# A kernel of two transformer blocks: the first modulation summed on TensorE by quarters of the channels

## Chip, cores and metric

One core of one Trainium2 chip. The metric is the device time of one execution in microseconds.

## What is computed

The input x (256 tokens by 1024 channels, float32) goes through two blocks: the first has a mixer of three branches (windowed attention, a gated recurrence, block attention) and a gated feed-forward layer, the second has differential attention, a Fourier mix, a dense feed-forward layer and eight experts. What the change touches is the very beginning:

```python
mod = silu(c) @ w_mod + b_mod          # c: 1024 numbers, w_mod: 1024 x 6144
shift_m, scale_m, ... = split(mod, 6)  # 1024 numbers each
h = rms_norm(x, norm_mix) * (1.0 + scale_m) + shift_m
z = h @ w_in                           # w_in: 1024 x 7424
```

So nothing of `z` can be finished before the first 2048 columns of `w_mod` (8 MB) have been read and multiplied by silu(c), while a partial sum of `z` over some input channels needs the scale and shift of these channels alone.

## The kernel before

There are 8 blocks of 128 channels, c = 0 to 7, and x lies transposed in `X`. Every weight matrix passes once through the chip, in slabs of 1 MB. SyncE issues all slab loads in one order (`st_order`, L535) into `raw` buffers. A load waits until its buffer's last slab is used. For a slab of a product (kind G, 1024 rows by 256 columns), ScalarE makes a rounded copy `whi` (`act_hi`, L1351), VectorE the rest `wlo = raw - whi` (`dve_lo`, L1969), and TensorE multiplies in three products (L663 to L665): 48 instructions for each slab of `w_in`. Three buffers of `whi` and `wlo` (NP = 3) let ScalarE and VectorE run up to three slabs ahead.

The modulation comes in slabs of kind M (512 rows by 512 columns, two to a group g of 512 outputs). `dve_mslabs` (L1991, L1994) multiplies the rows by silu(c) into an accumulator `macc`, and `pe_mods` (L741) sums that over the partitions into a column of the bank. `dve_mods` (L2012) adds the bias and puts it into `modT`. Groups 2 and 3 are the scale, groups 0 and 1 the shift. Only group 0 is summed by TensorE straight from the raw slab (`pe_mod_direct`, L755, with the 128x128 weights as the stationary operand and one column of silu(c) as the moving one).

The order of loads is: two slabs of group 2, x, two of group 3, two of group 0, two of group 1, then slabs 0, 1, 2 of `w_in`, then a slab of `w_in` and one of the next modulation in turn. On TensorE: transposes of x (L799), sums of squares for the norm (L768, L771), group 3 (L741), group 0 (L755), group 1, 14 multiplications that only keep the array busy (`spare`, L699), then `pe_mixer`: jobs 0 and 1 of `z` ("qa"), `pe_z_side(1)` (transposes L853, L859, the norm of job 0, L865), and from job 2 on one job, its side work and `pe_mods` in turn. Job 2 is "kv" (keys and values, 72 instructions), job 3 "qc" (48).

VectorE scales X (`scaled`, L2033), ScalarE adds the shift and rounds to `HH` (L1393), VectorE makes the rest `HL` (`low`, L2040). TensorE waits for `HL` of each block of channels (`xlo_done`). The loop of `dve_mixer` then makes `wlo` of slab t + 3, normalizes job t - 1 (L2245) and calls `dve_mslabs`.

## Time and profile before

| what | value |
|---|---|
| median of 3 runs | 2033.34 us (2030.17 to 2034.3) |
| the profiled execution | 2030.57 us, its span 2028.5 us |
| TensorE busy | 1980.4 us, 98% of the span |
| VectorE, ScalarE busy | 1702.0 us, 1257.4 us |
| read from memory | 585.89 MB, 289 GB/s over the span |

The span goes from the first to the last instruction. The profiled execution has its own time, 2.1 us over its span. Slabs count as 1 MB = 1.0486 million bytes here.

### The profile page before, as it was taken

The page shows a single profiled execution, that of the slowest core. Times are in us where ns is not written, and L with a number is a line of the kernel's source. Part 1 is how long each engine was busy: PE and PEld are TensorE (multiplying, and loading weights), DVE is VectorE, ACT ScalarE, POOL GpSimd, SP SyncE. Part 2 cuts the span into 40 slices and gives each one's busy share as a digit, 9 for nine tenths or more (in the row PEclk, how much of TensorE's full clock was granted, in tenths as well). Part 3 has the DMA queues.
Part 4 walks back from the last instruction along what each step waited for, and adds up shares of the span by engine and source line. Part 5 has one row for each costly group of instructions (what it writes and reads, how often), then busy time and mean ns, then how long its engine had stood idle before and what let it go on. Part 6 is the DMA issues. An engine that isn't in the chain of part 4 may idle for free.

```text
span 2028.5 us, 32745 instructions
## 1 busy us (share of the span) xinstructions
PE 1980.4 (98%) x13665; PEld 1771.3 (87%) x13665; DVE 1702.0 (84%) x1874; ACT 1257.4 (62%) x1269; POOL 39.5 (2%) x77
## 2 busy tenths in 40 slices
PE   7999999999999999999999999999999999999997
PEld 6889999999879899999878888888888888888886
DVE  6797888998786778887479898898988989898997
ACT  3469735654344554343367777777777777777775
POOL 3010000000000000000000000000000000000000
PEclk8999999999999999999999999999999999999999
DMA  9974876878643459999259999999999999999994
GB/s 310 302 248 138 264 235 224 263 235 277 219 165 105 146 194 332 320 322 324 84 208 368 368 354 371 350 374 361 362 361 355 369 352 370 367 354 369 368 372 158
DMA packets 337577, 589.16 MB, mean 290 GB/s; under 512 B 10518, under 2 KB 150316, under 8 KB 337425
## 3 DMA queue, kind: packets, MB, share of 16 engines
q1 hardware_dynamic: 333776, 580.70, 81.6%
q0 software_dynamic: 3008, 5.78, 1.0%
q8 instruction: 111, 1.82, 0.4%
q10 hardware_dynamic: 640, 0.52, 0.1%
q14 instruction: 42, 0.34, 0.1%
HBM read 585.89 MB, written 1.07 MB: 289 GB/s over the span
## 4 chain that ended last, share of the span: by engine, by line
PE 86%; DVE 8%; issue 3%; ACT 2%; DMA 1%; SPq 0%; DVEq 0%; ACTq 0%
PE bk L669 15%; PE bk L671 15%; PE bk L670 15%; PE bk L663 10%; PE bk L664 10%; PE bk L665 10%; DVE wlo L1969 2%; DVE macc L1994 2%; PE bk L1214 1%; ACT whi L1351 1%; DMA raw<-in_w_mod 1%; DVE uc L2349 1%; PE bk L1263 1%; PE bk L1126 1%; PE bk L725 1%
## 5 line engine op out<-in xcount | busy, mean ns | idle before, releaser
L1969 DVE TENSOR_TENSOR wlo<-raw,whi 128x2048 fp32r<-128x2048 f32 x477 | 1080.3, 2267 | 204.5 <-ACT whi L1351 203.2
L1351 ACT CAST whi<-raw 128x2048 fp32r<-128x2048 f32 x477 | 903.7, 1895 | 376.6 <-PE bk L671 249.0
L663 PE MATMUL bk<-HH,whi 128*128 128x256 f32 x1480 | 420.6, 284 | 0.9 <-DVE KC L2245 0.4
L664 PE MATMUL bk<-HL,whi 128*128 128x256 f32 x1480 | 410.4, 277 | 0.0
L665 PE MATMUL bk<-HH,wlo 128*128 128x256 f32 x1480 | 409.0, 276 | 0.0
L669 PE MATMUL bk<-whi,xh 128*128 128x512 f32 x896 | 354.4, 396 | 0.0
L671 PE MATMUL bk<-wlo,xh 128*128 128x512 f32 x896 | 349.3, 390 | 0.0
L670 PE MATMUL bk<-whi,xl 128*128 128x512 f32 x896 | 349.0, 390 | 0.0
L663 PEld LDWEIGHTS bk<-HH,whi 128*128 128x128 f32 x1480 | 276.9, 187 | 6.6 <-issue 3.8
L664 PEld LDWEIGHTS bk<-HL,whi 128*128 128x128 f32 x1480 | 279.6, 189 | 1.1 <-issue 0.7
L665 PEld LDWEIGHTS bk<-HH,wlo 128*128 128x128 f32 x1480 | 276.9, 187 | 0.0
L1994 DVE SCALAR_TENSOR_TENSOR macc<-raw,csil,macc 128x512 f32<-128x512 f32 x273 | 205.0, 751 | 10.2 <-DMA raw<-in_w_mod 1.8
L671 PEld LDWEIGHTS bk<-wlo,xh 128*128 128x128 f32 x896 | 168.2, 188 | 35.8
L669 PEld LDWEIGHTS bk<-whi,xh 128*128 128x128 f32 x896 | 168.3, 188 | 34.2 <-DVE wlo L1969 1.3
L670 PEld LDWEIGHTS bk<-whi,xl 128*128 128x128 f32 x896 | 168.4, 188 | 33.4
L669 PE MATMUL bk<-whi,tth 128*128 128x512 f32 x448 | 174.5, 390 | 0.7 <-DVE wlo L1969 0.7
L671 PE MATMUL bk<-wlo,tth 128*128 128x512 f32 x448 | 174.4, 389 | 0.0
L670 PE MATMUL bk<-whi,ttl 128*128 128x512 f32 x448 | 174.3, 389 | 0.0
L663 PE MATMUL bk<-FH,whi 128*128 128x256 f32 x400 | 113.2, 283 | 2.1 <-DVE wlo L1969 2.1
L664 PE MATMUL bk<-FL,whi 128*128 128x256 f32 x400 | 111.6, 279 | 0.0
L665 PE MATMUL bk<-FH,wlo 128*128 128x256 f32 x400 | 111.1, 278 | 0.0
L669 PEld LDWEIGHTS bk<-whi,tth 128*128 128x128 f32 x448 | 84.1, 188 | 18.5 <-DVE wlo L1969 1.1
(378 smaller groups left out, 2465.2 us busy)
## 6 DMA issues: line engine op xcount, KB each, us to landing
raw<-in_moe_w SPq DMA_DIRECT2D x334, 1024.0 KB, 6.5
raw<-in_ada_w SPq DMA_DIRECT2D x56, 1024.0 KB, 5.6
raw<-in_ff_w SPq DMA_DIRECT2D x40, 1024.0 KB, 5.9
raw<-in_w_in SPq DMA_DIRECT2D x29, 1024.0 KB, 5.5
raw<-in_w_mod SPq DMA_DIRECT2D x24, 1024.0 KB, 5.7
raw<-in_w_up SPq DMA_DIRECT2D x22, 1024.0 KB, 5.1
raw<-in_attn_w_qkv SPq DMA_DIRECT2D x12, 1024.0 KB, 5.6
raw<-in_w_branch SPq DMA_DIRECT2D x8, 1024.0 KB, 5.2
```

Of the source, the lines that this page charges most:

```text
L663: pe.matmul(o, sh, mh, start=start, stop=False, skip_group_check=True)
L664: pe.matmul(o, sh, ml, start=False, stop=False, skip_group_check=True)
L665: return pe.matmul(o, sl, mh, start=False, stop=stop, skip_group_check=True)
L669: pe.matmul(o, sh, mh, start=start, stop=False, skip_group_check=True)
L670: pe.matmul(o, sl, mh, start=False, stop=False, skip_group_check=True)
L671: return pe.matmul(o, sh, ml, start=False, stop=stop, skip_group_check=True)
L725: pe.matmul(o, xh[:, k, c], h[:, k, :], start=(k == 0), stop=False)
L1126: t = pe.matmul(u.t[:, m * S:(m + 1) * S], FN[:, tb, g + m, part * 128:part * 128 + 128], fcs[:, 256 + tb * 512 + part * 256:512 + tb * 51 ...
L1214: t = pe.transpose(u.t[:, j * 128:(j + 1) * 128], HB[s_ % 2][:, j * 128:(j + 1) * 128], ident)
L1351: act.copy(halves_at(q, g)[0], raw[q.slot[i]][:, :n]).then_inc(q.hi_done.mark(g), 1)
L1969: dve.tensor_tensor(low, raw[q.slot[i]][:, :n], high.bitcast(F), ALU.subtract).then_inc(q.taken.mark(i), 1)
L1994: t = dve.scalar_tensor_tensor(out=acc[:, :], in0=v[:, j, :], scalar=sc, in1=acc[:, :], op0=ALU.mult, op1=ALU.add)
```

## The change

`w_mod`'s first 2048 columns are now read in eight slabs of 1024 rows by 256 columns (kind D), as `w_in` is: quarter q holds the scale (w = 0) and the shift (w = 1) of channel blocks 2q and 2q + 1. x is loaded ahead of all slabs, and slab q of `w_in` between quarters q and q + 1, for q = 0, 1, 2. TensorE sums each slab (`pe_rows`): eight multiplications with silu(c), repeated over 32 columns (`c32`), as the stationary operand and 256 columns of the slab as the moving one; they write to four groups of 32 partitions in turn. ScalarE copies the bank (128x512) to `rowsum`, TensorE turns it into columns (`pe_rows_turn`, 16 multiplications), VectorE adds the two halves and the bias, and each quarter's scale, shift, `HH` and `HL` are made at once. TensorE does partial sums of jobs 0, 1 and 2 over the channel blocks there are (`part(t, k0, k1)`) between the quarters. Job 2 is now "qc" and "kv" is job 3. 16 multiplications of `spare` stand ahead of the slab (1, 0), the 14 ahead of job 0 are gone, and so is the sum of the first four groups of modulation on VectorE. The diff, cut to its core (what the new code replaces in `act_start` and `dve_start` is left out for the most part):

```diff
+        rowsum = macc[2:4]
+        c32, pick = sb("c32", [128, 8, 32]), sb("pick", [128, 1])
...
-        zjob = [("qa", 0, 0), ("qa", 1, 256), ("kv", 0, 512), ("qc", 0, 2816), ("qc", 1, 3072), ("kc", 0, 3328),
+        zjob = [("qa", 0, 0), ("qa", 1, 256), ("qc", 0, 2816), ("kv", 0, 512), ("qc", 1, 3072), ("kc", 0, 3328),
...
-        first = [s for g in (2, 3, 0, 1) for s in mslabs(wmod, g, 0)]
-        st_order = first + order[0:3]
+        quarter = [[("D", (q, w), gslabs(wmod, 8, c0 + 256 * q, None)[0][2], 8, 256) for w, c0 in enumerate((D, 0))] for q in range(4)]
+        st_order = quarter[0] + order[0:1] + quarter[1] + order[1:2] + quarter[2] + order[2:3] + quarter[3]
...
-        early = (6, 7, 8, 0, 1, 2, 3, 6, 8)
+        early = (6, 7, 0, 8, 6, 1, 7, 8, 2, 6, 7)
         for i, entry in enumerate(st_order):
-            st.add(entry, early[i] if i < 9 else (i - 9) % NR)
...
+            st.add(entry, early[i] if i < 11 else (i - 8) % NR)
+            if entry[0] == "D":
+                st.direct[entry[1]] = i
...
-            yield from sp_weights(st, 0, 2)
...
-            yield from sp_weights(st, 2, len(st.plan))
+            yield from sp_weights(st, 0, len(st.plan))
...
+        def pe_rows(q, w):
+
+            u = take(Z_T, "row", q, w)
+            i = st.direct[q, w]
+            v = raw[st.slot[i]][:, :].rearrange("p (k n) -> p k n", k=8)
+            if q == 0 and w == 0:
+                pe.wait_ge(*(yield from dve_step.of("c32")))
+            if q == 1 and w == 0:
+                spare(u.t[:, 0:128], 16)
+            pe.wait_ge(st.raw_in[st.slot[i]], 16 * st.use[i])
+            for k in range(8):
+                r, half = 32 * (k % 4), k // 4
+                t = pe.matmul(u.t[r:r + 32, half * S:(half + 1) * S], c32[:, k, :], v[:, k, :], start=True, stop=True, skip_group_check=True)
+            t.then_inc(st.summed.mark(i), 1)
             u.told = st.summed.now()
...
+        def pe_rows_turn(q, w):
+
+            u = take(Z_T, "first", q, w)
+            pe.wait_ge(*(yield from N.of("row", q, w)))
+            for half in range(2):
+                for j in range(2):
+                    for r in range(0, 128, 32):
+                        c = half * S + j * 128 + r
+                        t = pe.matmul(u.t[r:r + 32, 2 * half + j:2 * half + j + 1], rowsum[w][:, c:c + 32], pick[:, 0:1],
+                                      start=True, stop=True, skip_group_check=True)
+            t.then_inc(u.fill(), 1)
...
+            u = take(Z_T, "vec", 0)
+            pe.wait_ge(*(yield from N.of("vn", 0)))
+            pe.transpose(u.t[:, 0:128], vn[0][:, :], ident).then_inc(u.fill(), 1)
+            yield from pe_rows(0, 0)
             yield from pe_stats(Z_S, "x0", 4)
             yield from pe_stats(Z_S, "x0", 6)
-            yield from pe_mods(Z_T, -1, 2)
-            pe.wait_ge(*N.at["csil",])
-            pe_mod_direct(Z_T, 0)
-            yield from pe_mods(Z_T, -1)
+            yield from pe_rows_turn(0, 0)
+            yield from pe_rows(0, 1)
+            yield from pe_rows_turn(0, 1)
...
+            us, parts = [], []
+
+            def part(t, k0, k1):
+                if t == len(us):
+                    us.append(take(Z_G, "z", t))
+                    parts.append((yield from slab(st, ("z", zjob[t][2]))))
+                h, l, _ = parts[t]
+                for k in range(k0, k1):
+                    pe.wait_ge(*(yield from xlo_done.of("h0", k)))
                     for m in range(2):
                         cols = slice(m * 128, (m + 1) * 128)
-                        tt = three(u.t[:, m * S:(m + 1) * S], (h[:, k, cols], l[:, k, cols]), (HH[:, k, :], HL[:, k, :]),
+                        tt = three(us[t].t[:, m * S:(m + 1) * S], (h[:, k, cols], l[:, k, cols]), (HH[:, k, :], HL[:, k, :]),
                                    k == 0 and m == 0, k == 7)
-                tt.then_inc(st.slab_done.mark(t), 1)
-                u.told = st.slab_done.now()
+                if k1 == 8:
+                    tt.then_inc(st.slab_done.mark(t), 1)
+                    us[t].told = st.slab_done.now()
+
+            for q, between, behind in ((1, ((0, 0, 2),), ()), (2, ((0, 2, 4),), ((1, 0, 4),)),
+                                       (3, ((0, 4, 6), (1, 4, 6)), ((2, 0, 2), (0, 6, 8), (1, 6, 8), (2, 2, 5)))):
+                yield from pe_rows(q, 0)
+                yield from pe_rows_turn(q, 0)
+                for what in between:
+                    yield from part(*what)
+                yield from pe_rows(q, 1)
+                yield from pe_rows_turn(q, 1)
+                for what in behind:
+                    yield from part(*what)
             yield from pe_z_side(1)
+            yield from part(2, 5, 8)
+            yield from pe_z_side(2)
+            yield from pe_mods(Z_T, 2)
...
-                if t < 2:
+                if t < 3:
...
-            act.wait_ge(*(yield from B.full("vec", 0)))
-            u = B.at["vec", 0]
-            act.copy(vt[0][:, :], u.t[:, 0:128]).then_inc(u.sem, 1)
-            N.note(("vec", 0), u.drained())
...
-            yield from act_stat("x0")
-            yield from act_hi(st, 0)
...
+            act.wait_ge(*(yield from B.full("vec", 0)))
+            u = B.at["vec", 0]
+            act.copy(vt[0][:, :], u.t[:, 0:128]).then_inc(u.sem, 1)
+            N.note(("vec", 0), u.drained())
+            for q in range(4):
+                for w in range(2):
+                    if q:
+                        act.wait_ge(*(yield from B.full("first", q - 1, w)))
+                    act.wait_ge(*(yield from B.full("row", q, w)))
+                    u = B.at["row", q, w]
+                    act.copy(rowsum[w][:, :], u.t[:, :]).then_inc(u.sem, 1)
+                    N.note(("row", q, w), u.drained())
+                    if q == 0 and w == 0:
+                        yield from act_stat("x0")
+                act.wait_ge(*(yield from N.of("coeff", q, 1)))
+                for c in (2 * q, 2 * q + 1):
+                    act.wait_ge(*(yield from dve_step.of("t", "h0", c)))
+                    act.activation(HH[:, c, :], sqb[q % 3][:, c % 2 * S:c % 2 * S + S], AF.Identity,
+                                   bias=modT[0][:, c:c + 1]).then_inc(xhi_done.mark("h0", c), 1)
+                if q < 3:
+                    yield from act_hi(st, q)
...
+            dve.memset(pick[:, :], 0.0).then_inc(dve_step.mark("pick0"), 1)
+            dve.wait_ge(*dve_step.now())
+            for r in range(0, 128, 32):
+                dve.memset(pick[r:r + 1, :], 1.0).then_inc(dve_step.mark("pick"), 1)
...
+            for k in range(8):
+                dve.tensor_scalar(c32[:, k, :], one[:, 0:32], csil[:, k:k + 1], None, ALU.mult).then_inc(dve_step.mark("c32"), 1)
...
-            for c in range(6):
-                yield from scaled(c)
-            yield from dve_mslabs(st.gi[0])
-            yield from dve_lo(st, 0)
...
+            def summed(q, w):
+                c = 8 * (1 - w) + 2 * q
+                dve.wait_ge(*(yield from B.full("first", q, w)))
+                u, o = B.at["first", q, w], modT[0][:, c:c + 2]
+                dve.tensor_tensor(o, u.t[:, 0:2], vec("b_mod")[:, c:c + 2], ALU.add).then_inc(dve_step.mark("first"), 1)
+                dve.wait_ge(*dve_step.now())
+                dve.tensor_tensor(o, u.t[:, 2:4], o, ALU.add).then_inc(u.sem, 1)
+                dve.wait_ge(*u.drained())
+                N.note(("coeff", q, w), u.drained())
+
+            dve.wait_ge(*(yield from N.of("vec", 0)))
+            for q in range(4):
+                if q:
+                    yield from dve_lo(st, q - 1)
+                yield from summed(q, 0)
+                dve.scalar_tensor_tensor(out=nA[:, 2 * q:2 * q + 2], in0=modT[0][:, 8 + 2 * q:10 + 2 * q], scalar=1.0,
+                                         in1=vec("norm_mix")[:, 2 * q:2 * q + 2], op0=ALU.add, op1=ALU.mult).then_inc(dve_step.mark("A", "h0"), 1)
+                dve.wait_ge(*dve_step.now())
+                for c in (2 * q, 2 * q + 1):
+                    yield from scaled(c)
+                yield from summed(q, 1)
+                for c in (2 * q, 2 * q + 1):
+                    yield from low(c)
...
-                yield from dve_mslabs(st.gi[t + NP + 1])
+                if t:
+                    yield from dve_mslabs(st.gi[t + NP + 1])
                 if t >= 25:
                     for p in (2 * (t - 25), 2 * (t - 25) + 1):
                         yield from dve_split("o", p, OH, OL, O[:, 2 * p:2 * p + 2, :])
```

## Rows read from the trace of the kernel before

**Rows 1.** The page: the span, and busy time of TensorE (share, instructions).

```profile
span 2028.5 us, 32745 instructions
...
PE 1980.4 (98%) x13665; PEld 1771.3 (87%) x13665; DVE 1702.0 (84%) x1874; ACT 1257.4 (62%) x1269; POOL 39.5 (2%) x77
```

**Rows 2.** Windows (from:to, length, busy of each engine, clock, DMA share, GB/s).

```profile
0.00:60.00 60.00, 43.53 (x343) 40.06 (x344) 39.34 (x60) 24.58 (x36) 18.73 (x40) 0.86 0.95 320
60.00:100.00 40.00, 40.00 (x375) 36.30 (x375) 29.58 (x39) 18.18 (x22) 2.32 (x5) 1.00 0.89 291
```

**Rows 3.** Waits of TensorE from 60 us to the end: total, times, longest.

```profile
PE bk L779 <- DVE sqb L2278: 7.9, 4, 4.5
...
PE bk L741 <- ACT O L1447: 1.3, 1, 1.3
```

**Rows 4.** Timeline of TensorE: start, length, line, operation (us).

```profile
23.46 0.43 PE L741 MATMUL bk<-one,macc 128*32 128x1 f32 x32 [1.41 <-DVE macc L1994]
23.94 12.74 PE L755 MATMUL bk<-csil,raw 128*128 128x1 f32 x64
...
37.19 5.74 PE L699 MATMUL bk<-one,cst 128*128 128x128 f32 x28
42.69 0.36 PE L663 MATMUL bk<-HH,whi 128*128 128x256 f32 x1
...
54.10 0.49 PE L853 MATMUL bk<-cst,vn 128*128 128x128 f32 x3
...
57.24 1.13 PE L865 MATMUL bk<-sqb,cst 128*128 128x512 f32 x2 [1.26 <-ACT vt L1560]
```

**Rows 5.** Timeline of VectorE, the seventh slab of w_mod.

```profile
30.44 0.49 DVE L1991 TENSOR_SCALAR macc<-raw,csil 128x512 f32<-128x512 f32 x1 [3.56 <-DMA raw<-in_w_mod]
```

**Rows 6.** Timeline of ScalarE: the first slab of w_in, and its copies behind job 1.

```profile
36.16 1.90 ACT L1351 CAST whi<-raw 128x2048 fp32r<-128x2048 f32 x1 [13.09 <-DMA raw<-in_w_in]
...
56.58 0.60 ACT L1560 COPY vt<-bk 128x128 f32<-128x128 f32 x3
```

**Rows 7.** Windows at the start, columns as in Rows 2.

```profile
24.00:30.00 6.00, 6.00 (x34) 6.00 (x34) 2.75 (x8) 0.00 (x0) 0.00 (x0) 0.59 1.05 385
32.00:42.00 10.00, 10.00 (x76) 9.95 (x77) 7.55 (x11) 3.40 (x5) 0.00 (x0) 0.50 1.10 348
46.00:50.00 4.00, 4.00 (x35) 3.85 (x34) 4.00 (x3) 2.88 (x3) 0.00 (x0) 1.00 0.13 28
```

**Rows 8.** Chain of waits at 86 to 89 us: start, length, line.

```profile
86.21 0.86 PE bk L865 x2
87.07 1.01 PE bk L872 x8
88.08 0.36 PE bk L741 x32
88.45 0.31 PE bk L663
```

**Rows 9.** Lines, 0 to 60 us: count, busy, mean ns of one, idle before.

```profile
L2040 DVE SCALAR_TENSOR_TENSOR HL<-sqb,mod_m,HH 128x256 fp32r<-128x256 f32 x8 | 3.5, 482 | 1.2 <-ACT HH L1393 1.2
...
L1393 ACT ACTIVATE HH<-sqb,mod_m 128x256 fp32r<-128x256 f32 x8 | 3.4, 498 | 2.4 <-DVE mod_m L2012 2.4
...
L1420 ACT COPY X<-bk 128x512 f32<-128x512 f32 x4 | 2.3, 572 | 4.6 <-PE bk L799 4.6
...
L2012 DVE TENSOR_TENSOR mod_m<-bk,vt 128x4 f32<-128x4 f32 x4 | 0.6, 157 | 1.4 <-PE bk L741 1.4
```

**Rows 10.** Windows about two later falls of the clock, columns as in Rows 2.

```profile
523.00:527.00 4.00, 0.00 (x0) 0.00 (x0) 3.96 (x6) 0.00 (x0) 0.78 (x2) 0.98 1.05 344
527.00:534.00 7.00, 6.52 (x24) 5.84 (x25) 2.68 (x7) 2.60 (x6) 2.40 (x5) 0.52 0.98 239
971.00:973.00 2.00, 0.03 (x1) 0.06 (x1) 1.93 (x5) 0.00 (x0) 0.00 (x0) 1.00 0.35 35
973.00:978.00 5.00, 5.00 (x22) 4.42 (x23) 1.93 (x6) 2.24 (x6) 0.00 (x0) 0.66 0.56 201
```

More of the change, by code:

```diff
@@ L441, in build @@
             s_ = i % (NR + NX)
-            st.add(entry, (s_ + first_moe - 9) % NR if s_ < NR else s_)
-        mlist = [(0, g, None, "start") for g in (2, 3, 0, 1)]
-        for (which, g), _, when in mplan:
-            mlist.append((which, g, when))
+            st.add(entry, (s_ + first_moe - 8) % NR if s_ < NR else s_)
+        mlist = [(which, g, when) for (which, g), _, when in mplan]
         last_slab = {(t[0], t[1]): i for i, (kind, t, *_) in enumerate(st.plan) if kind == "M" and t[2] == 1}
@@ L451, in build @@
         mnum = {(d, g): n for n, (d, g, *_) in enumerate(mlist)}
-        gaps = {"start": -1, "x1": 40.5, "x3": 90.5, "x4": 134.5}
+        gaps = {"x1": 40.5, "x3": 90.5, "x4": 134.5}
         due = lambda n, slot: n < len(mlist) and gaps.get(mlist[n][3], mlist[n][3]) <= slot
@@ L744, in pe_mods @@
                 pmod[0] += 1
-        def pe_mod_direct(ring, g):
-            u = take(ring, "mod", pmod[0])
-            for k0 in range(2):
-                i = st.direct[g, k0]
-                w = raw[st.slot[i]]
-                pe.wait_ge(st.raw_in[st.slot[i]], 16 * st.use[i])
-                for k in range(4):
-                    for j in range(4):
-                        t = pe.matmul(u.t[:, j:j + 1], w[:, k * 512 + j * 128:k * 512 + j * 128 + 128], csil[:, 4 * k0 + k:4 * k0 + k + 1],
-                                      start=(k0 + k + j == 0), stop=(k0 == 1 and k == 3), skip_group_check=True)
-                t.then_inc(st.summed.mark(i), 1)
-            u.told = st.summed.now()
-            pmod[0] += 1
+        def pe_rows(q, w):
[11 more added lines that the diff above has]
+            t.then_inc(st.summed.mark(i), 1)
+            u.told = st.summed.now()
+        def pe_rows_turn(q, w):
[8 more added lines that the diff above has]
+            t.then_inc(u.fill(), 1)
         def pe_stats(ring, name, c, halves=False):
@@ L789, in pe_start @@
             pe.transpose(u.t[:, 0:24], crow[:, :], ident[0:24, 0:24]).then_inc(u.fill(), 1)
-            u = take(Z_T, "vec", 0)
-            pe.wait_ge(*(yield from N.of("vn", 0)))
-            pe.transpose(u.t[:, 0:128], vn[0][:, :], ident).then_inc(u.fill(), 1)
-            yield from pe_mods(Z_T, -1, 1)
             pe.wait_ge(*(yield from N.of("xn")))
@@ L1423, in act_start @@
             act.wait_ge(*(yield from dve_step.of("eps")))
-            yield from act_stat("x0")
-            yield from act_hi(st, 0)
-            half = act_modulate("h0", HH, 0, 0, sqb)
-            for k in range(2):
-                for need in half:
-                    if need[0] == "pace":
-                        if need[2] == 3:
-                            break
-                    else:
-                        yield need
-                if k == 0:
-                    yield from act_hi(st, 1)
-            yield from act_hi(st, 2)
+            act.wait_ge(*(yield from B.full("vec", 0)))
[19 more added lines that the diff above has]
+                    yield from act_hi(st, q)
         def act_head(h, step):
@@ L2083, in dve_start @@
-            yield from dve_lo(st, 0)
-            yield from dve_mods(-1, 3)
-            for c in range(2):
-                yield from low(c)
-                yield from scaled(6 + c)
-            for c in range(2, 4):
-                yield from low(c)
-            yield from dve_mods(-1)
-            for c in range(4, 8):
-                yield from low(c)
-            yield from dve_lo(st, 1)
-            yield from dve_lo(st, 2)
+            dve.memset(pick[:, :], 0.0).then_inc(dve_step.mark("pick0"), 1)
@@ new lines, in dve_start @@
+            dve.wait_ge(*dve_step.now())
+            for r in range(0, 128, 32):
+                dve.memset(pick[r:r + 1, :], 1.0).then_inc(dve_step.mark("pick"), 1)
+            dve.wait_ge(*(yield from N.of("cst")))
+            dve.wait_ge(*(yield from N.of("csil")))
+            for k in range(8):
+                dve.tensor_scalar(c32[:, k, :], one[:, 0:32], csil[:, k:k + 1], None, ALU.mult).then_inc(dve_step.mark("c32"), 1)
+            scaled, low = modulation("h0", X, HH, HL, 0, 0, 0, sqb)
```

16 lines of the change are left out of this document (removed).

## The prediction

> **What bounds the kernel now.** I read the page first: TensorE is busy for 98% of the span [rows 1]. So a change at the start is worth what it lets TensorE do earlier, provided the later work keeps its pace. The windows by stage come next. In the first 60 us TensorE is busy for 43.5 us, at a mean clock of 0.86; from 60 to 100 us it is busy all the time [rows 2]. The waits after 60 us name one long place, before the norms (L779), 4.5 us at most, and small ones such as L741's 1.3 us [rows 3]. None of them is for a transfer by name. They hang on VectorE and ScalarE work that TensorE itself releases, so I take it that they move with it.
>
> Then the timeline of the start. Group 3 of the modulation is summed in 0.43 us at 23.46; group 0, summed straight from the slab with one moving column, takes 12.74 us; the 14 spare multiplications take 5.74 us; and `z` begins at 42.69 [rows 4]. Jobs 0 and 1 end at 54.10, so a job of 48 instructions costs (54.10 - 42.69) / 2 = 5.70 us. Behind them TensorE waits 1.26 us, and the norm of job 0 starts at 57.24 [rows 4]. It takes 0.86 us [rows 8], so job 2 can begin at 58.10.
>
> The transfers are the other bound. x and seven slabs are there at 30.44 at the earliest that VectorE can show [rows 5], and the first slab of `w_in`, the tenth MB, is there at 36.16 [rows 6]. The windows show that the queue is full: 385 GB/s while only slabs of 512 columns travel, 348 while slabs of 256 columns do, and 28 at 46 to 50 us, when the loads wait for buffers [rows 7]. A wide slab so costs 1.0486 / 0.385 = 2.72 us and a narrow one 3.01.
>
> **The change, part by part.** The comparison point is the start of "kv", with jobs 0, 1 and "qc", and the norms of jobs 0 and 1, done. Before, "kv" comes first: swapped, that point would be 58.10 + 5.70 + 0.86 = 64.66 us.
>
> *Arrival.* The last modulation slab (3, 1) is the twelfth MB, and eight slabs turn from wide to narrow: 36.16 + 2 x 3.01 + 8 x 0.29 = 44.5 us; slab (3, 0) is there at 41.5, slab (2, 0) at 32.5. x first costs nothing, as its work (16 transposes, four squares) lies long before. Each buffer is used again three to five slabs later and its sum is short, so SP's queue should not stall. The copies `whi` and `wlo` of slabs 0 to 2 lie between the quarters on ScalarE (1.90 us [rows 6]) and VectorE, in the 9 us that a quarter takes to arrive.
>
> *One sum (`pe_rows`).* The trace has none with four groups of 32 partitions and 256 columns. The nearest is L872: four multiplications of 256 columns to two groups of 64 partitions, in 1.01 us. One such multiplication in full width takes 0.43, half of a 512-column one [rows 8]; four in a row would be 1.72. So two groups did run beside each other: 2 x 0.43 and 0.15 for the pipeline. With four groups, eight multiplications are again 2 x 0.43 + 0.15 = 1.0 us; that is the low end. Half as good (two at a time) is 1.9 us, no overlap 3.4 + 0.15 = 3.6 us. I take 1.0, since L872 differs by the number of groups only.
>
> The Trainium skill ("TensorE: Matmul & The Clock Gate", Part 3) gives 2.38 times for three column groups. By an estimate from that page alone, four groups would lose a fifth and a sum would be about 1.2 us. Four sums lie on the path behind 32.5 us, so the gain would be 0.9 us smaller. No run here shows that.
>
> *One turn.* ScalarE's copy of a 128x512 bank is 0.57 us [rows 9] and about 0.1 for the semaphores; 32 records of L741's kind take 0.43 [rows 4]. Going back to full width costs 0.31 - 0.12 = 0.2 us for the first product (the 0.12 is 5.70 / 48) [rows 8].
>
> *The path behind slab (3, 0), with the clock at its upper level.* 41.5, sum 42.5, copy 43.2, turn 43.6, switch 43.8. Two quarter jobs (2 x 1.43) end at 46.65, so slab (3, 1) has been there for 2 us. Sum 47.65, copy 48.3, turn 48.75, switch 48.95. Job 2's first quarter ends at 50.4. Meanwhile the two additions (0.16 each [rows 9]), `HH` and `HL` (0.50 and 0.48 [rows 9]) of block 6 end at about 50.2: covered. If that cover were gone it would cost up to 1.4 us. The rests of jobs 0 and 1 end at 53.2 and job 2's next 3/8 at 55.4. The side work to the end of `rows` is 57.24 - 1.26 - 54.10 = 1.9 us [rows 4], so 57.3. ScalarE has done z0's square, slab 3, z1's square and slab 4 by 56.8 and one copy of `vecs` by 57.4 (0.60 x3 of them as before [rows 6]): TensorE waits 0.1 instead of 1.26. Norm 58.3, job 2's rest 60.4, norm 61.3. The gain is 64.66 - 61.3 = 3.4 us.
>
> *The clock.* Two things in the trace say that it won't stay up. It was down at 32 to 42 us, under multiplications of one column [rows 7]. And later, after 4 us and after 2 to 3 us without work, the rows show it going down and staying at its lower level (1.2 of 2.4 GHz) for some 6 and some 3 us of work [rows 10]. In the new start TensorE is done with quarter 1 at about 29.5 us and has nothing until slab (2, 0) at 32.5. So I expect it low when quarter 2 begins. Each us of work at half clock adds up to half a us: 1.6 to 2.9 us late. Quarter 2 has 8.4 us of work and copies in 9 us, so 0.6 us is absorbed, and 1.0 to 2.3 stay. I take the middle, 1.7. The gain is then 3.4 - 1.7 = 1.7 us.
>
> *What is freed.* VectorE loses six slabs of sums before 36 us (0.49 and three times 0.76 each and so on), but it is not late there: nothing gained. *What is added:* `c32` and `pick`, some 13 small operations of 0.16 us, before the first slab is there: nothing. *What follows:* slabs 3 and 4 arrive behind (3, 1), at 47.5 and 53.2, before ScalarE wants them. VectorE no longer takes the slab of group 4 in its round 0; it takes two in round 1, 6.2 us in one piece, with slab 5's `wlo` and the load that waits for the buffer queued behind it. These end at about 68 us, 8 us ahead of job 5. In the stage of 60 to 100 us VectorE has 10.4 us to spare [rows 2]. Nothing should be late.
>
> **The rivals.** (a) *The clock stays up*, because the sums and the partial jobs are work enough: 3.4 us gained, and up to 5 if the narrow slabs come faster than 3.01 us. For it: 16 spare multiplications stand ahead of quarter 1. Against it: rows 10. Time 2029.9, down to 2028.
>
> (b) *The four groups don't run beside each other.* Then a sum is 3.6 us. Each of the four sums from 32.5 us on is 2.6 longer, less the 0.6 of slack: 9.8 us late against 3.4 gained, so 6.4 slower: 2039.7. The point from which it decides: a sum of 1.0 + (1.7 / 4) = 1.4 us uses up what my forecast gains. Against it is L872, for it only that no row has four groups and 256 columns.
>
> (c) *The gain doesn't get through.* The round of VectorE with two modulation slabs, or a buffer that comes free late, makes TensorE wait at jobs 5 to 7, and the start ends where it did: 2033.3, or up to 2 us more. For it: 28 GB/s at 46 to 50 us shows how buffers can hold the loads up. Against it: 8 us of slack by my count.
>
> (d) *More is gained than the sum*, 4 to 9 us: if the wait chains at 100 to 140 us get slack from a start that leaves the loads further ahead (the hole at 46 to 50 us is filled). The largest wait there is 1.3 us [rows 3], so it would need shifts that I don't see.
>
> **How the numbers follow.** The profiled execution took 2030.57 us, 2.8 below the median of 2033.34; the sum gives 2030.57 - 1.7 = 2028.9 for it and 2031.6 against the median. I give 2031.6. Chances: forecast (1.0 to 2.3 gained) 0.47, (a) 0.22, (b) wholly or in part 0.10, (c) 0.13, (d) 0.08. What a measurement of this kernel can tell from no change is about 0.2%, 4.1 us. The runs of before differ by 4 us among each other, so a shift of the median by 1 to 2 us lies on top of every case. Faster by over 0.2%: (d), nearly half of (a), a fifth of the forecast: 0.26. Slower by over 0.2%: (b) and a little of (c) and of the rest: 0.13. Same 0.61. The range leaves out the ends of (b) and (d): 2025.5 to 2037.
>
> **What would show it.** `pe_rows` in 1.0 us for 16 records; slab (3, 1) there at 44 to 45 us; a granted clock of 0.5 from about 32 us for 3 to 6 us; the last turn at 48.5 to 51; "kv" beginning at 61 to 64. After it, TensorE without waits to 100 us. Wrong: sums of 2 us and more at full clock, a wait of SP's queue for a sum, slabs 3 to 6 late, or a clock that stays low past 45 us.

## The result, and the profile after

The changed kernel takes 2034.14 us (median of 20 runs, 2031.63 to 2038.86), the kernel before 2031.70 us in the same comparison (20 runs, 2027.58 to 2034.53). The ratio is 1.0015, with a 95% interval of 1.0009 to 1.0022: about 3 us slower (2.4 by the two medians). The forecast was 2031.6 us against a median of 2033.34, that is 1.7 us faster. The change is small, as forecast, but it goes the other way.

The profiled execution of the kernel after took 2037.5 us (span 2035.9), 3.4 us above its median; that of before took 2030.57. So their difference (6.9 us) is not the change's price. I use the two traces for what happens up to 160 us, and the medians for the sum.

The page of after, its span and busy time of TensorE (before: [rows 1]):

```profile
span 2035.9 us, 33231 instructions
PE 1984.3 (97%) x13893; PEld 1768.2 (87%) x13893; DVE 1689.2 (83%) x1878; ACT 1261.8 (62%) x1277; POOL 39.4 (2%) x77
```

The windows of after, for the first three stages and for two short stretches (columns as in [rows 2]; before, the first two stretches are in [rows 2]):

```profile
0.00:60.00 60.00, 44.06 (x584) 34.30 (x585) 22.36 (x59) 27.79 (x42) 17.60 (x38) 0.94 0.93 295
60.00:100.00 40.00, 37.15 (x331) 32.77 (x330) 30.46 (x36) 18.49 (x23) 3.23 (x6) 0.96 0.95 305
100.00:150.00 50.00, 48.27 (x469) 44.78 (x468) 45.22 (x114) 31.36 (x64) 6.17 (x11) 0.97 0.82 264
...
54.00:60.00 6.00, 5.93 (x41) 4.45 (x40) 3.24 (x2) 5.67 (x9) 0.00 (x0) 1.00 0.04 13
64.00:70.00 6.00, 6.00 (x53) 6.00 (x53) 5.72 (x8) 3.13 (x3) 2.18 (x4) 1.00 0.53 97
```

The second line is the result in short. From 60 to 100 us TensorE was busy all the time before [rows 2]; now it is busy for 37.15 of 40 us, and its mean granted clock is 0.96. The last two lines show the transfers: nearly none from 54 to 60 us (13 GB/s), and few from 64 to 70 (97 GB/s: nothing up to 66 us, then 89 and 201 GB/s in stretches of 2 us). In the trace of before the same two stretches were these:

```profile
54.00:60.00 6.00, 4.74 (x28) 2.93 (x27) 4.38 (x5) 4.92 (x9) 1.06 (x2) 1.00 1.07 367
64.00:70.00 6.00, 6.00 (x48) 5.52 (x48) 0.64 (x1) 3.10 (x5) 2.19 (x4) 1.00 0.84 287
```

TensorE's waits in after, from 20 to 60 us and from 60 to 160 us (what it waited for; us in total, times, longest):

```profile
PE bk L767 <- ACT macc L1455: 5.1, 6, 0.9
PE bk L755 <- DMA raw<-in_w_mod: 3.0, 1, 3.0
...
PE bk L660 <- DVE O L2285: 2.9, 1, 2.9
PE bk L738 <- ACT O L1476: 1.3, 1, 1.3
```

The first two belong to the new start, and the prediction had them. The third is new and was not foreseen: a job of `z` (its multiplications are L660 to L662 here) waits for a bank until VectorE has applied a norm (`O`, L2285). Before had no wait there. The fourth is in both kernels (before: L741 in [rows 3]).

How late the work is behind this wait is read from VectorE's `wlo` of slab 9, a step that every kernel has, first in before and then in after: 3.6 us.

```profile
96.65 2.29 DVE L1969 TENSOR_TENSOR wlo<-raw,whi 128x2048 fp32r<-128x2048 f32 x1 [1.94 <-ACT whi L1351]
...
100.23 2.29 DVE L1998 TENSOR_TENSOR wlo<-raw,whi 128x2048 fp32r<-128x2048 f32 x1 [1.94 <-ACT whi L1376]
```

**The start.** The timeline of TensorE in after (columns as in [rows 4]):

```profile
31.77 1.25 PE L755 MATMUL bk<-raw,c 128*32 128x256 f32 x16 [3.02 <-DMA raw<-in_w_mod]
33.84 0.60 PE L767 MATMUL bk<-pick,macc 128*32 128x1 f32 x32 [0.83 <-ACT macc L1455]
...
37.23 1.94 PE L755 MATMUL bk<-raw,c 128*32 128x256 f32 x16
40.02 0.43 PE L767 MATMUL bk<-pick,macc 128*32 128x1 f32 x32 [0.85 <-ACT macc L1455]
...
48.66 1.07 PE L755 MATMUL bk<-raw,c 128*32 128x256 f32 x16
50.58 0.43 PE L767 MATMUL bk<-pick,macc 128*32 128x1 f32 x32 [0.85 <-ACT macc L1455]
...
62.60 1.02 PE L874 MATMUL bk<-sqb,cst 128*128 128x512 f32 x2
```

A sum (L755) takes 1.07 us, and 1.94 us where the clock is at its lower level (the row at 37.23). A turn (L767) takes 0.43, and 0.60 at the lower level. Behind every sum stand 0.85 us in which ScalarE copies the bank. The last line is the norm of job 1: 62.60 + 0.86 = 63.46 us is the point where "kv" can begin, 1.2 us ahead of the 64.66 of before.

**Where the gain goes.** TensorE from the end of job 4, with the norm of "kv", into job 5 (rows in between left out):

```profile
78.93 0.59 PE L874 MATMUL bk<-sqb,cst 128*128 128x256 f32 x2
82.37 0.39 PE L660 MATMUL bk<-HH,whi 128*128 128x256 f32 x1 [2.85 <-DVE O L2285]
...
83.42 0.28 PE L662 MATMUL bk<-HH,wlo 128*128 128x256 f32 x1
...
84.00 0.42 PE L660 MATMUL bk<-HH,whi 128*128 128x256 f32 x1
...
86.77 0.41 PE L661 MATMUL bk<-HL,whi 128*128 128x256 f32 x1
```

It stands for 2.85 us, and a little over one us after it goes on, the same multiplication takes 0.41 instead of 0.28 us, for 3.4 us. The granted clock of 84 to 86 us is 0.50: half the pace, some 1.6 us more. What it waits for, on ScalarE (first group) and VectorE (second; the x2 at 56.76 is slabs 3 and 4):

```profile
77.42 1.91 ACT L1376 CAST whi<-raw 128x2048 fp32r<-128x2048 f32 x1 [4.61 <-DMA raw<-in_w_in]
79.24 0.68 ACT L1403 ACTIVATE rst<-bk,eps_c 128x512 f32<-128x512 f32 x1
...
56.76 4.57 DVE L1998 TENSOR_TENSOR wlo<-raw,whi 128x2048 fp32r<-128x2048 f32 x2 [3.79 <-ACT whi L1376]
62.84 0.48 DVE L2020 TENSOR_SCALAR macc<-raw,csil 128x512 f32<-128x512 f32 x1
63.36 5.54 DVE L2023 SCALAR_TENSOR_TENSOR macc<-raw,csil,macc 128x512 f32<-128x512 f32 x7
68.82 2.28 DVE L1998 TENSOR_TENSOR wlo<-raw,whi 128x2048 fp32r<-128x2048 f32 x1
74.49 0.49 DVE L2020 TENSOR_SCALAR macc<-raw,csil 128x512 f32<-128x512 f32 x1 [2.72 <-DMA raw<-in_w_mod]
79.36 2.29 DVE L1998 TENSOR_TENSOR wlo<-raw,whi 128x2048 fp32r<-128x2048 f32 x1 [2.03 <-ACT whi L1376]
81.57 0.74 DVE L2285 SCALAR_TENSOR_TENSOR O<-bk,vt,rst 128x512 f32<-128x512 f32 x1
```

Read it from the end. The bank of job 2 comes free when VectorE's L2285 at 81.57 has read it. On VectorE that stands behind slab 6's `wlo` at 79.36; on ScalarE the norm's root (79.24) stands behind slab 6's `whi` at 77.42; and that copy had waited 4.61 us for slab 6 itself. So the norm had to wait for a transfer with which it has nothing to do, because it is queued, on two engines, behind work that uses what is transferred.

Why is slab 6 late? The issues of SP, and GpSimd's loads beside them:

```profile
59.08 0.37 SPq L533 DMA_DIRECT2D raw<-in_w_in  x1
65.71 0.37 SPq L533 DMA_DIRECT2D raw<-in_w_mod  x1
66.12 0.51 SPq L533 DMA_DIRECT2D raw<-in_w_in  x1
...
64.95 2.18 POOL L589 DMA_DIRECT2D bi<-bias_rows  x4 [3.77 <-DMA bias_rows<-rrow]
```

The two issues at 65.71 and 66.12 (a modulation slab, and slab 6) stood at 56.05 and 59.04 in SP's timeline of before. The first needs the buffer of a modulation slab that VectorE now sums only in its round 1 (62.84 and 63.36 in the rows above). Slab 5 at 59.08 needs the buffer of slab 3, whose `wlo` (56.76) waits for ScalarE's copy, which is queued behind the end of job 0: at 54.3 us instead of 48.4 (42.69 + 5.70). So between 54 and 60 us next to nothing travels. And the loads that go out at 65.7 meet GpSimd's four loads of the bias tables.

### The profile page after: what moved, and what is told of

Read it like the earlier page. It is cut to its first block, busy times and chain, and to the rows that moved or that the text cites. A ratio compares the mean times of both kernels' runs of the same rounds, so it can differ in the third digit from the quotient of the medians.

```text
span 2035.9 us, 33231 instructions
## 1 busy us (share of the span) xinstructions
PE 1984.3 (97%) x13893; PEld 1768.2 (87%) x13893; DVE 1689.2 (83%) x1878; ACT 1261.8 (62%) x1277; POOL 39.4 (2%) x77
## 3 DMA queue, kind: packets, MB, share of 16 engines
HBM read 585.89 MB, written 1.07 MB: 288 GB/s over the span
## 4 chain that ended last, share of the span: by engine, by line
PE 84%; DVE 8%; issue 3%; ACT 3%; DMA 1%; SPq 0%; DVEq 0%; ACTq 0%
PE bk L666 15%; PE bk L668 15%; PE bk L667 15%; PE bk L660 10%; PE bk L661 9%; PE bk L662 9%; DVE wlo L1998 2%; DVE macc L2023 2%; ACT whi L1376 1%; PE bk L1239 1%; PE bk L1288 1%; PE bk L1151 1%; DMA raw<-in_w_mod 1%; DVE uc L2390 1%; PE bk L1202 1%
## 5 line engine op out<-in xcount | busy, mean ns | idle before, releaser
L660 PE MATMUL bk<-HH,whi 128*128 128x256 f32 x1480 | 423.3, 286 | 3.8 <-DVE O L2285 2.9
L662 PE MATMUL bk<-HH,wlo 128*128 128x256 f32 x1480 | 412.4, 279 | 0.0
L660 PEld LDWEIGHTS bk<-HH,whi 128*128 128x128 f32 x1480 | 279.3, 189 | 9.8 <-issue 3.6
L662 PEld LDWEIGHTS bk<-HH,wlo 128*128 128x128 f32 x1480 | 279.5, 189 | 0.0
L2023 DVE SCALAR_TENSOR_TENSOR macc<-raw,csil,macc 128x512 f32<-128x512 f32 x252 | 189.2, 751 | 7.8
L660 PE MATMUL bk<-FH,whi 128*128 128x256 f32 x400 | 112.5, 281 | 2.1 <-DVE wlo L1998 2.1
L662 PE MATMUL bk<-FH,wlo 128*128 128x256 f32 x400 | 110.6, 276 | 0.0
```

What stands on the lines that cost most here:

```text
L660: pe.matmul(o, sh, mh, start=start, stop=False, skip_group_check=True)
L662: return pe.matmul(o, sl, mh, start=False, stop=stop, skip_group_check=True)
L2023: t = dve.scalar_tensor_tensor(out=acc[:, :], in0=v[:, j, :], scalar=sc, in1=acc[:, :], op0=ALU.mult, op1=ALU.add)
```

## The experiments

Theory A: the loss is a matter of order. The norm of job 2 is queued behind slab 6's work on ScalarE and VectorE; put ahead of it, the wait is gone and the gain is there. Theory B: the loss is a matter of lateness. The loads of 56 to 66 us are late since VectorE no longer sums a modulation slab in its round 0; the bank is only the place where it first shows. Beside them stand three smaller suspects: the clock, the buffer that slab 5 takes from slab 3, and GpSimd's bias loads.

All runs, each beside the kernel before on the same chip. "Norm 1" is the start of the norm of job 1 (in terms of before, 64.66 - 0.86 = 63.80 us). "Slab 9" is the start of VectorE's `wlo` of that slab (96.65 in before). The recorded expectations call the same step slab 8's; counted from the first slab of `w_in` as slab 0, it is the tenth, slab 9. The column before it is the way from norm 1 to this step (96.65 - 63.80 = 32.9 in before): it leaves out how well the start of that one execution went, and shows what is lost behind it. "Wait" is what TensorE waits in all from 60 to 100 us:

| kernel | median us | ratio to before | norm 1 | wait | norm 1 to slab 9 | slab 9 |
|---|---|---|---|---|---|---|
| after | 2034.14 | 1.0015 [1.0009, 1.0022] | 62.60 | 2.9 | 37.6 | 100.2 |
| e1_round0 | 2031.47 | 1.0002 [0.9993, 1.0011] | 63.51 | 1.2 | 34.3 | 97.8 |
| e2_norm_first | 2032.51 | 1.0008 [0.9999, 1.0017] | 64.04 | 2.4 | 37.0 | 101.0 |
| e3_sum_early | 2029.63 | 0.9994 [0.9985, 1.0003] | 63.73 | 0 | 32.9 | 96.6 |
| e4_bias_later | 2030.95 | 1.0004 [0.9993, 1.0014] | 63.70 | 0 | 33.7 | 97.4 |
| e11_apart_only | 2031.63 | 0.9996 [0.9988, 1.0005] | 64.76 | 0 | 32.9 | 97.7 |
| e5_spare | 2032.16 | 1.0004 [0.9995, 1.0013] | 61.49 | 2.2 | 35.5 | 97.0 |
| e8_early_spare | 2028.61 | 0.9985 [0.9976, 0.9993] | 62.10 | 0 | 32.9 | 95.0 |
| e10_apart_spare | 2028.81 | 0.9990 [0.9981, 0.9998] | 62.13 | 0 | 32.9 | 95.0 |
| e13_pairs | 2028.42 | 0.9992 [0.9983, 1.0001] | 61.38 | 0 | 32.9 | 94.3 |
| e12_filled | 2026.88 | 0.9981 [0.9971, 0.9991] | 60.49 | 0 | 32.9 | 93.4 |

The times and ratios come from 10 to 20 runs of each kernel, the other columns from its one profiled execution. After loses 37.6 - 32.9 = 4.8 us (unrounded) behind norm 1; e3, e11, e8, e10, e13 and e12 lose nothing there.

### e1_round0: VectorE sums a modulation slab in round 0 again

```
-                if t:
-                    yield from dve_mslabs(st.gi[t + NP + 1])
+                yield from dve_mslabs(st.gi[t + NP + 1])
```

> Theory A (the bank): TensorE waits 2.85 us ahead of job 5 for the bank of job 2, whose norm stands on ScalarE and VectorE behind slab 6, and slab 6 came late; the wait makes the clock fall (3.1 us at half, 1.6 us). So some 4.4 us of the loss are there. Here VectorE sums the modulation slab in round 0 again (between slab 3 and slab 4), as before the change. By A the next modulation load is issued at 62 instead of 65.7 us, slab 6 lands 3 us earlier and most of the wait goes: 3 to 4.4 us faster than the changed kernel, about 1 us faster than the kernel before. Rival R1 (VectorE): slab 4's low part and the norm of job 0 come 3.1 us later and TensorE waits for them instead: no gain, the changed kernel's 3 us over the kernel before. Rival R2 (nothing local: falls of the clock by chance): no change either, and the wait stays.

The ratio falls to 1.0002; most of the loss is gone. The modulation load goes out at 62.74 and slab 6 at 64.94, 3.0 and 1.2 us earlier than in after, the wait ahead of job 5 is 1.2 us, and the clock does not fall behind it. So that one line carries most of the price: 2.6 us against after by the ratios, where 3 to 4.4 were expected. Not all: behind norm 1 the work is still 1.5 us late, 1.2 of it in the wait.

### e2_norm_first: the norm of job 2 ahead of slab 6

```
+                if t == 3:
+                    act.wait_ge(*(yield from B.full("norm", 2)))
+                    yield from act_rstd(("z", 2), B.at["norm", 2], 512, 64)
                 yield from act_hi(st, t + NP)
```

and the same on VectorE: in round 3 the scaling L2285 ahead of `dve_lo`.

> One part alone, the order in round 3: the norm of job 2 (rstd on ScalarE, the scaling on VectorE) ahead of slab 6's high and low part; the loads are left as they are. By theory A the wait ahead of job 5 goes (2.85 us) and with it the fall of the clock (1.6 us): 4.4 us faster than the changed kernel, 1 to 1.5 us faster than the kernel before. By theory B (the loads themselves are late, the bank is only where it shows first) TensorE waits for slab 6's parts at job 6 instead, some 2 us, and the gain is 2 us or less. By R2 nothing changes.

TensorE's waits from 60 to 100 us in this kernel:

```profile
PE bk L881 <- DVE ss L2257: 2.4, 1, 2.4
```

The wait for the bank is gone, as both theories say, and another one of 2.4 us stands 7 us later (it ends at 89.8), before the scores' first step (L881), again with a fall of the clock (0.50 from 92 to 94 us). It is not at job 6, where theory B had put it. What releases it is the norm of "kv", and on VectorE this stands behind slab 7's `wlo`:

```profile
86.92 2.29 DVE L2001 TENSOR_TENSOR wlo<-raw,whi 128x2048 fp32r<-128x2048 f32 x1 [1.12 <-ACT whi L1376]
```

ScalarE's copy of slab 7 had waited 3.83 us for the transfer. Slab 9 is at 101.0, 0.8 later than in after; as this start was 1.4 us later, 0.7 of the 4.8 us lost behind norm 1 came back. The ratio of 1.0008 can't be told from that of after. So A is refuted as the cause: it names the place at which the lateness is handed on, and when that is mended, the next one in the queue hands it on. B holds.

### e3_sum_early: the modulation slab is summed right at the end of the start

```
                 for c in (2 * q, 2 * q + 1):
                     yield from low(c)
+            yield from dve_mslabs(st.gi[3] + 2)
```

VectorE was idle for 3.79 us there (the row at 56.76 above).

> VectorE sums the first modulation slab of the mixer in the idle stretch before slab 3's low part (it has 3.8 us there, the sum takes 3.1). The buffer is free at 57 instead of 66 us, so the load behind slab 5 is issued at about 59.5 instead of 65.7 us. By A and B both the hole in the loads at 60 to 66 us closes, slab 6 lands about 6 us earlier and the wait is gone: 4.4 us faster than the changed kernel, 1 to 1.5 us faster than the kernel before. By R2 no change. If the sum delays slab 3's low part (it shouldn't), the load of slab 5 comes later by as much.

SP's issues and the window of 64 to 70 us in this kernel:

```profile
60.60 0.58 SPq L533 DMA_DIRECT2D raw<-in_w_mod  x1
62.47 0.37 SPq L533 DMA_DIRECT2D raw<-in_w_in  x1
...
64.00:70.00 6.00, 6.00 (x49) 5.60 (x48) 5.21 (x7) 3.65 (x4) 2.18 (x4) 1.00 1.08 374
```

The two loads go out 5.1 and 3.7 us earlier than in after, before GpSimd's loads; the stretch moves 374 GB/s instead of 97, with the same four bias loads in it (POOL 2.18). No wait is left from 60 to 100 us. Against after the median is some 4 us lower by the ratios (0.9994 to 1.0015), for one line. But it can't be told from before: slab 9 is at 96.64, where before had 96.65, and at 155 us both are at 155.3. The start of this execution gained nothing (norm 1 at 63.73 against 63.80).

### e5_spare and e8_early_spare: the clock kept up

```
-            if q == 1 and w == 0:
-                spare(u.t[:, 0:128], 16)
+            if q and w == 0:
+                spare(u.t[:, 0:128], (16, 11, 0)[q - 1])
```

The 11 spare multiplications fill the 3.0 us in which TensorE waits for slab (2, 0). e5 is after with this alone, e8 has e3's line too.

> 11 spare multiplications (0.21 us each at full clock, 2.3 us) in the 3.0 us in which TensorE waits for slab (2, 0), and none added elsewhere, so that the clock doesn't fall at 32.5 us (it was at half until 38.6, 6 us, which is 2 to 3 us of work late less what the wait for the next slab absorbs). By the prediction's clock term the start of kv comes 1.0 to 2.3 us earlier (61 to 62.5 instead of 63.5). What the whole gains depends on theory A: the bank wait is released by loads that move with job 0's end, so by A the gain gets through, 1 to 2 us; if the loads are bound by something else, the wait grows by as much and the time stays.

> Both: the first modulation slab of the mixer summed in VectorE's idle stretch before slab 3's low part (as in e3_sum_early, which ended all waits of TensorE from 60 to 100 us and put the work at 155 us exactly where the kernel before has it), and 11 spare multiplications ahead of slab (2, 0) (as in e5_spare, which kept the clock up to 60 us and brought slab 3's low part 1.2 us forward). Theory B (the loads set the pace, released by the end of job 0): the two add up, slab 8's low part at about 95.4 us against 96.6 and 96.7 before, 1.2 us faster than e3_sum_early and 2 to 2.5 us faster than the kernel before (ratio 0.9988 to 0.999). Rival R3 (the loads are full by then): the 1.2 us are lost again to a wait for a slab before 100 us, ratio as of e3_sum_early, 0.9994.

In both the granted clock is 1.00 from 0 to 60 us. e5 reaches norm 1 at 61.49, and still waits 2.2 us ahead of job 5: an earlier start doesn't cure the late loads. But the wait did not grow by what the start gained, and this time the clock did not fall behind it (1.00 from 60 to 100 us): slab 9 comes 3.2 us earlier than in after. e8 has neither loss (windows of e8, 0 to 60 and 60 to 100 us):

```profile
0.00:60.00 60.00, 45.04 (x608) 35.64 (x608) 25.43 (x63) 28.03 (x42) 17.99 (x39) 1.00 0.94 295
...
60.00:100.00 40.00, 40.00 (x373) 36.29 (x372) 32.14 (x42) 19.60 (x24) 3.39 (x7) 1.00 1.01 337
```

Slab 9 is at 95.02, 1.6 us ahead of e3 and of before, and the ratio 0.9985 has its interval below one. The change can gain, once both its prices are removed.

### e10_apart_spare and e11_apart_only: slab 5 in a buffer of its own

```
-            st.add(entry, early[i] if i < 11 else (i - 8) % NR)
+            st.add(entry, early[i] if i < 11 else 8 if i == 15 else (i - 8 - (i > 15)) % NR)
```

Slab 5 no longer waits for slab 3's `wlo`. The loads behind it move on by one buffer (the same is done for the experts' slabs): the modulation slab now takes slab 3's buffer, and slab 6 that of the modulation slab summed in round 1. e10 is e8 with this, e11 is after with this alone.

> As e8_early_spare, and the load of slab 5 goes to the ninth raw buffer (free since slab (2, 1) was summed), so that it doesn't wait for slab 3's low part: the loads go on at 54 to 60 us, where they stand still in the changed kernel (0 to 38 GB/s). By theory B no load is late any more: no wait of TensorE to 100 us. If e8_early_spare has none either, the same time, ratio 0.9988; if it still has one (R3), this one is faster by that wait.

> The changed kernel with the load of slab 5 alone moved to the ninth raw buffer, nothing else. This fills the hole of the loads at 54 to 60 us; the modulation slab is still summed in round 1 on VectorE (66 us). Theory B1 (the hole, released by job 0's late end, is the root): the modulation slab behind slab 5 is issued at about 59 instead of 65.7 us, VectorE doesn't wait for it (2.7 us in the changed kernel), slab 6 lands 3 us earlier, and the wait of 2.85 us ahead of job 5 is gone or under 0.5 us: 3 to 4 us faster than the changed kernel. Theory B2 (the late sum of the modulation slab is the root, as its buffer takes slab 6): slab 6 is issued at 66 us as before and lands at 72 to 75; the wait stays at 1.5 us or more, and the gain is 1 to 2 us.

The windows of 54 to 60 us, first in e10, then in e11:

```profile
54.00:60.00 6.00, 5.92 (x39) 4.14 (x37) 4.91 (x4) 5.72 (x9) 0.36 (x1) 1.00 0.60 180
...
54.00:60.00 6.00, 5.99 (x52) 5.77 (x50) 2.00 (x3) 4.04 (x6) 0.00 (x0) 1.00 0.50 163
```

The hole is half filled (180 and 163 GB/s instead of 13 in after and 25 in e8). In e10 this changes nothing: slab 9 is at 95.04 against 95.02. In e11 it ends the wait ahead of job 5: the modulation slab goes out at 61.20 instead of 65.71, so that slab 6, though issued at 67.84, 1.7 us later than in after, is copied at 74.84, 2.6 us earlier. So the hole costs only where the modulation slab is summed late as well; either remedy is enough. The start of e11's profiled execution was the slowest of all (norm 1 at 64.76), and nothing was lost behind it.

### e4_bias_later: GpSimd's bias loads held back

```
             pool.wait_ge(arrived, n)
+            pool.wait_ge(*(yield from st.slab_done.of(4)))
             for h in range(16):
```

> The changed kernel with GpSimd's four loads of the bias tables (0.5 MB in 1 KB rows, at 65 to 70 us, where the windows show 89 and 201 GB/s at a DMA share of 0.68 and 0.90) held back until job 4 is done (79 us). Theory B4 (they collide with the late slabs: the modulation slab took 8.8 us from issue to landing, slab 6 11 us, against 6 before): the slabs issued at 65.7 and 66.1 us land 2 us earlier, the wait ahead of job 5 falls from 2.85 to about 1 us, and the whole gains 2 to 3.5 us. Rival: the transfers themselves are what fills the time, and the wait stays within 0.5 us. The tables are needed at 99 us at the earliest, so holding them costs nothing.

Window of 64 to 70 us in this kernel:

```profile
64.00:70.00 6.00, 6.00 (x49) 5.63 (x48) 5.68 (x10) 3.63 (x4) 0.00 (x0) 1.00 0.47 138
```

No bias load lies in this stretch (POOL 0.00). The two SP loads go out as late as in after (66.81 and 67.22), but arrive in time: ScalarE copies slab 6 at 75.03, 7.8 us after its issue, where it was 11.3 in after. There is no wait ahead of job 5, and slab 9 is at 97.4 instead of 100.2 (0.8 us late, counted from norm 1). So the bias loads are a third cause, and removed alone they end the wait too.

### e12_filled and e13_pairs: what is left of the start

e12 is e8 with one channel block's products put between each sum and its turn in quarters 2 and 3, over ScalarE's copy:

```
+                for w, mid, end in ((0, inside, between), (1, inside1, behind)):
+                    yield from pe_rows(q, w)
+                    for what in mid:
+                        yield from part(*what)
+                    yield from pe_rows_turn(q, w)
```

> e8_early_spare with products put between each sum and its turn in quarters 2 and 3 (one channel block's six, 0.71 us), where TensorE waits 0.85 us for ScalarE's copy of the bank. In e8_early_spare TensorE has no wait for a slab behind 33 us, so these four waits, 3.4 us, are on the path. Each product group put there costs one more change of the array's width there and back, some 0.25 us, and the turns come some 0.1 us later. Theory (TensorE is the path behind slab (2, 0)): 4 x (0.71 - 0.25) = 1.8 us earlier at job 3, slab 8's low part at 93.2 us against 95.0, ratio about 0.9977 against the kernel before. Rival (slab (3, 1)'s chain to HL 6 and 7, or its arrival, is the path): the waits turn up ahead of the last parts of jobs 0 and 1, and the time stays that of e8_early_spare, 0.9985.

e13 is e8 with the eight multiplications of a sum in another order:

```
-            for k in range(8):
+            for k in (0, 4, 1, 5, 2, 6, 3, 7):
```

> e8_early_spare with the order of the eight multiplications of a sum changed alone: two to the same 32 partitions follow each other (blocks 0, 4, 1, 5, 2, 6, 3, 7 instead of 0 to 7), the work is the same. If the four groups run beside each other because neighbours in the queue are in different groups (the prediction's reading of the rows of two groups), a sum now takes 1.7 to 2.1 us instead of 1.07, four sums behind slab (2, 0) cost 2.5 to 4 us, and the whole is 2.5 to 4 us slower than e8_early_spare, about as the kernel before or 1 us slower. Rival: the array sorts it out, or the sum is bound by something else: 1.07 us and the same time.

A sum and its turn in e12, then a sum in e13 (the timeline of TensorE):

```profile
35.64 1.07 PE L755 MATMUL bk<-raw,c 128*32 128x256 f32 x16
37.56 0.43 PE L767 MATMUL bk<-pick,macc 128*32 128x1 f32 x32
...
41.16 1.09 PE L755 MATMUL bk<-raw,c 128*32 128x256 f32 x16
```

In e12 the turn no longer waits for the copy: of six waits of 0.85 us in the start, two are left. TensorE waits 0.7 and 0.9 us for the slabs (2, 0) and (3, 0) instead, so the loads now bound the start in part. Norm 1 is at 60.49 and slab 9 at 93.39 (93.2 expected), 1.6 us ahead of e8. 2026.88 us, ratio 0.9981 [0.9971, 0.9991], is the lowest found; its interval overlaps with that of e8. In e13 two neighbours go to the same group of partitions, and the sum takes 1.09 instead of 1.07 us. So the short sum does not hang on neighbours being in different groups, which was my reading; that reading is refuted. No run sends all eight multiplications to one group, so it is not shown whether the four groups are needed, or whether multiplications of 32 columns are this short in any case.

## Why the prediction was wrong, point by point

**The steps of the start were right in kind.** A sum took 1.07 us where 1.0 was taken; "no overlap" (rival (b)) is out. The Trainium skill ("TensorE: Matmul & The Clock Gate", Part 3) gives a speedup of 2.38 for three column groups. By an estimate from that page, four groups give 2.38 / 3 x 4 = 3.17, and a sum is 3.44 / 3.17 = 1.08 us; the prediction's 1.2 counted 0.15 us for the pipeline on top. The trace agrees with the 1.08 (1.07). A turn took 0.43, the first full-width product 0.39 instead of 0.28; the copy with its semaphores 0.85, where 0.67 was taken. The clock fell in quarter 2, from about 33 to 39 us, as forecast from [rows 10]. "kv" could begin at 63.46, inside the 61 to 64 given.

**Two terms of the start were mis-sized.** Where the clock stayed up (e5, e8, e10, e13) norm 1 is at 61.38 to 62.13, mean 61.8; the sum had 60.4. So the gain at the upper clock against 63.80 is 2.0 us, not 3.4. The sum for slab (3, 0) begins at 41.5 on average in these four, as the prediction had it; the 1.4 us are lost behind it. Two copies at 0.18 more and two sums at 0.07 more are 0.5 of it; the rest is a stand of 0.8 to 1.1 us right behind the turn of slab (3, 0), for which the profile names no releaser. In e12 a stand of 0.56 us falls between two records of that very turn, where the code has no wait, so it isn't a wait for another engine there; its cause is open. In the six kernels without the added spares norm 1 lies between 62.60 and 64.76, mean 63.7: the clock costs 1.9 us on average (1.7 was taken), and the execution of after is the luckiest of the six. So the mean gain at "kv" is about 0.1 us instead of the 1.7 of the forecast (the 63.80 itself rests on one execution of before). That fits e1, e3, e4 and e11, which have little or no wait, and all have a ratio that can't be told from 1. So the forecast would have been 1.6 us too good even without any wait.

**The step that failed, and turned the sign, is the one headed "What follows".** It says of the two modulation slabs in VectorE's round 1: "These end at about 68 us, 8 us ahead of job 5 ... Nothing should be late." The time was right (the `wlo` behind them begins at 68.82). The slack was counted for the wrong thing. I measured it from slab 5's `wlo` to the job that multiplies slab 5. But the buffer that this round frees is refilled by a load that stands ahead of slab 6 on SP's queue; slab 6's copies stand on ScalarE and VectorE ahead of the norm of job 2; and TensorE needs that norm's bank in job 5. Along this chain the slack was negative:

- the modulation load and slab 6 go out at 65.71 and 66.12 instead of 56.05 and 59.04;
- slab 6 is there at 77.4, 11.3 us after its issue, and 7.8 after it where GpSimd's loads are held back (e4);
- the norm's scaling starts at 81.57, and TensorE has stood since 79.5.

Three things had to meet: the skipped round 0 (undone in e1, replaced in e3), slab 5 behind the end of job 0 (e11), and the bias loads (e4). Each one taken away alone ended the wait or cut it to 1.2 us, and behind norm 1 at most 1.5 of the 4.8 us stayed lost. The prediction named rival (c), "a buffer that comes free late makes TensorE wait at jobs 5 to 7", and gave it 0.13; it named for it the low rate at 46 to 50 us in [rows 7], and against it the 8 us. It priced it as the gain lost and up to 2 us more. It left out that a wait of this length takes the clock down with it, though [rows 10] show just that.

**The sum.** In the two traces: 1.2 gained at "kv", 2.85 lost in the wait, about 1.6 in the clock behind it: 3.3 us late, and slab 9 is late by 100.23 - 96.65 = 3.6. With the mean gain of 0.1 it would be 4.4. The ratio says 3.0, the medians 2.4. In e5 the same wait came without a fall of the clock, so this term isn't there every time; that fits a time below the full sum, but how often it falls was not measured.

**Rivals.** (a), the clock stays up: no, except where spares were added, and then e8 gains 3.0 us by its ratio (2.2 by the two medians). (d) had no sign in any trace.

**The chances.** Faster 0.26, same 0.61, slower 0.13: the interval of 1.0009 to 1.0022 lies mostly within 0.2%, so the case with the largest chance came true, but by an account that had 0.13, rival (c). That the time stayed within 0.2% is no merit of the forecast's mechanism.

## What to carry to other kernels

When a step on a helper engine is moved to a later round, follow the buffer that it frees: the load that reuses it, what is queued behind that load, and what is queued behind that load's users. The slack of the moved step is that of the last link, not that of its own result. A wait of 2 to 3 us on TensorE cost half as much again through the clock here (1.6 on 2.85 us; in e5 nothing was added), so a start that is faster by 1 to 2 us is worth nothing if it makes one such wait. A change can work at its own place and still lose; here one line more, in idle time of VectorE, and 11 spare multiplications turned 3 us slower (ratio 1.0015) into 2 to 3 us faster (0.9985 in e8; e10 and e13, which are e8 with one thing more, have 0.9990 and 0.9992).

## What the runs showed of the hardware

**Eight multiplications to four groups of 32 partitions take a third of their time in full width, in both orders tried.** 1.07 us for 128x256 in 16 records, 1.09 with two neighbours in the same group; in full width eight would be 3.4 (8 x 0.43 [rows 8]).

**The clock can fall after a shorter stand than [rows 10] show, and not every time.** Both kernels have the wait of 1.3 us that [rows 3] name; it ends at 140.7 us in before (L741) and at 144.3 in after (L738). In the profile of before the granted clock was 1.00 all the way from 134 to 152 us; in after it was this:

```profile
142.00:150.00 8.00, 6.69 (x69) 6.22 (x69) 5.87 (x16) 4.37 (x11) 2.95 (x5) 0.79 0.83 243
```

It fell right behind this wait in e2, e5 and e12 too, and not in the other eight. It costs about 1.5 us where it happens: from slab 9's `wlo` to the eighth `wlo` behind it the time is 60.1 to 60.2 us in these four, and 58.4 to 59.0 in the others. What decides it is open.

**A pace that differs between executions.** From about 745 to 910 us TensorE is busy all the time at a clock of 1.00, in all profiles. But in those of after, e1, e3 and e13 the same work takes some 3.1 us longer than in the others. The same two `wlo` steps of VectorE, first in before, then in after:

```profile
745.61 2.28 DVE L1969 TENSOR_TENSOR wlo<-raw,whi 128x2048 fp32r<-128x2048 f32 x1
...
908.91 2.29 DVE L1969 TENSOR_TENSOR wlo<-raw,whi 128x2048 fp32r<-128x2048 f32 x1 [0.23 <-ACT whi L1351]
...
750.40 2.28 DVE L1998 TENSOR_TENSOR wlo<-raw,whi 128x2048 fp32r<-128x2048 f32 x1
...
916.80 2.29 DVE L1998 TENSOR_TENSOR wlo<-raw,whi 128x2048 fp32r<-128x2048 f32 x1 [0.34 <-ACT whi L1376]
```

163.30 us lie between them in before, and 166.40 in after. In e8 it is 163.30 again, in e3 166.41. The code of this stretch is the same and no wait is named. As e3 and e8 differ only at the start, it isn't tied to the edit that is studied; its cause is open. It is 3.1 of the 6.9 us by which the two profiled executions lie apart, while the medians lie 2.4 us apart; a single profiled time therefore says little here.
